# The low half of split weights made by GpSimd instead of an accumulating DMA, and the indexer's dots taken one head at a time

## What is computed

```python
for l in range(DEPTH):                      # 2 layers, x: (1, 512, 1024)
    x = x + 0.5 * swiglu(rms_norm(x, ffn1_norm[l]), ffn1_gate[l], ffn1_up[l], ffn1_down[l])   # 1024 -> 2816 -> 1024
    h = rms_norm(x, mix_norm[l])
    aq, ak, av, iq, ik, iw, pu, mq = jnp.split(h @ w_in[l], IN_OFFSETS, axis=-1)
    # A: sparse attention, 8 heads x 64. The indexer (4 heads x 64) scores every key:
    #    score[t,s] = sum_h iw[t,h]/2 * relu(iq[t,h] . ik[s] / 8), s <= t
    #    each query keeps the 128 keys of the largest score and attends to them
    # B: causal pooling over trailing windows 2, 4, 8, 16, a small map per group
    # C: attention of 4 heads to 256 memory tokens
    x = x + jnp.concatenate([y_attn, y_pool, y_mem], axis=-1) @ w_out[l]
    x = x + 0.5 * swiglu(rms_norm(x, ffn2_norm[l]), ffn2_gate[l], ffn2_up[l], ffn2_down[l])
```

## Time and profile before

| | us |
|---|---|
| median of 3 runs | 1982.85 (1980.84 to 1983.37) |
| the profiled execution's own time | 1983.37 |
| its span in the profile | 1981.4 |
| TensorE busy | 1948.7 (98%) |
| ScalarE busy | 1086.5 (55%) |
| VectorE busy | 617.1 (31%) |
| GpSimd busy | 350.7 (18%) |
| w_lo<-raw: DMAs issued, us to landing | 328, 5.7 |

### The profile page before, as it was taken

One profiled execution on the slowest core, in us unless ns is written; L12 is line 12 of the kernel. 1 busy time (PEld: TensorE's weight loads), 2 busy tenths in 40 slices (PEclk: granted clock), 3 DMA queues, 4 the chain that ended last, 5 costly groups with the idle time before them and its releaser, 6 DMA issues.

```text
span 1981.4 us, 27709 instructions
## 1 busy us (share of the span) xinstructions
PE 1948.7 (98%) x9256; PEld 1571.9 (79%) x9256; DVE 617.1 (31%) x1180; ACT 1086.5 (55%) x1393; POOL 350.7 (18%) x404
## 2 busy tenths in 40 slices
PE   6999999999999999999999999999999999999999
PEld 4888888886768888888878888888767688888887
DVE  3222200367662322220052222004676532222101
ACT  6655543563584655553375565336546666565432
POOL 1111111111431111111111111111116111111111
PEclk9999999999999999999999999999999999999999
DMA  7988888887336888888878888888762379888886
GB/s 217 218 188 192 195 190 194 190 192 176 83 87 144 195 188 190 193 194 194 195 170 200 189 186 199 196 195 200 185 155 54 87 170 206 194 197 189 195 195 180
DMA packets 97799, 354.54 MB, mean 179 GB/s; under 512 B 11000, under 2 KB 11256, under 8 KB 97472
## 3 DMA queue, kind: packets, MB, share of 16 engines
q0 software_dynamic: 47232, 171.99, 48.7%
q1 hardware_dynamic: 49824, 178.84, 27.5%
q10 hardware_dynamic: 672, 2.80, 0.4%
HBM read 179.52 MB, written 2.10 MB: 92 GB/s over the span
## 4 chain that ended last, share of the span: by engine, by line
PE 97%; DMA 1%; ACT 1%; issue 1%; DVE 0%; SPq 0%; DVEq 0%; ACTq 0%; POOLq 0%
PE bank L453 95%; PE bank L806 2%; DMA w_lo<-raw 1%; DMA x<-x_t 0%; ACT w_lo L920 0%; ACT prob L1066 0%; DVE pt L336 0%; ACT a_hi L1082 0%; ACT t L1066 0%; DVE t L1323 0%; DVE x L1150 0%; DVE z L1277 0%; ACT pt L1059 0%; ACT mv L1046 0%; DVE yt L1341 0%
## 5 line engine op out<-in xcount | busy, mean ns | idle before, releaser
L919 ACT ACTIVATE w_hi<-raw 128x1024 fp32r<-128x1024 f32 x329 | 349.0, 1061 | 645.5 <-PE bank L453 630.8
L453 PE MATMUL bank<-h_hi,w_hi 128*128 128x512 f32 x1664 | 654.6, 393 | 15.9 <-ACT h_hi L891 13.9
L453 PE MATMUL bank<-h_hi,w_lo 128*128 128x512 f32 x1664 | 649.5, 390 | 5.6 <-DMA w_lo<-raw 5.6
L453 PE MATMUL bank<-h_lo,w_hi 128*128 128x512 f32 x1664 | 632.9, 389 | 0.0
L385 POOL DMA_DIRECT2D w_lo<-raw x328 | 283.5, 866 | 1589.6 <-ACT w_lo L920 1549.7
L453 PEld LDWEIGHTS bank<-h_hi,w_hi 128*128 128x128 f32 x1664 | 313.3, 188 | 97.5 <-ACT h_hi L891 15.3
L453 PEld LDWEIGHTS bank<-h_hi,w_lo 128*128 128x128 f32 x1664 | 313.3, 188 | 71.3 <-DMA w_lo<-raw 6.1
L453 PEld LDWEIGHTS bank<-h_lo,w_hi 128*128 128x128 f32 x1664 | 312.4, 188 | 65.5 <-issue 1.2
L920 ACT ACTIVATE w_lo<-raw 128x1024 fp32r<-128x1024 f32 x329 | 343.5, 1044 | 0.0
L453 PE MATMUL bank<-a_hi,w_hi 128*128 (+2 forms) x864 | 334.1, 387 | 0.0
L453 PE MATMUL bank<-a_lo,w_hi 128*128 (+2 forms) x864 | 332.8, 385 | 0.0
(11 more groups left out here) (138 smaller groups left out, 1273.9 us busy)
## 6 DMA issues: line engine op xcount, KB each, us to landing
raw<-weights SPq DMA_DIRECT2D x332, 512.0 KB, 4.6
w_lo<-raw POOLq DMA_DIRECT2D x328, 512.0 KB, 5.7
x<-x_t SPq DMA_DIRECT2D x4, 512.0 KB, 7.3
mem<-mem_t ACTq DMA_DIRECT2D x2, 1024.0 KB, 7.1
out_t<-x SPq DMA_DIRECT2D x8, 256.0 KB, 2.1
const<-consts SPq DMA_DIRECT2D x1, 505.5 KB, 10.1
spread_in<-spreads ACTq DMA_DIRECT2D x2, 216.0 KB
wpool<-pool_w ACTq DMA_DIRECT2D x2, 128.0 KB, 7.0
```

What stands on the lines that cost most here:

```text
L453: return nc.tensor.matmul(out_, lhsT, rhs, start=start, stop=stop, skip_group_check=True)
L919: nc.scalar.activation(w_hi[:, s], raw[:, s], ACT.Copy).then_inc(w_hi_done, 1)
```

## The change

w_lo is no longer made by a negating ScalarE pass and an accumulating DMA, but by one GpSimd `tensor_tensor` that subtracts w_hi from raw. One semaphore `w_ready` counts the slots in order, in place of four. The dots of the indexer are no longer paired nor put between the v blocks: they run head by head, before project_v(2), in two banks, and from the third on each waits for a relu. ROUNDS_AT is gone: each of the ten evacuations is followed by one round, and FIRST_ROUNDS is 6 instead of 2.

```diff
-ROUNDS_AT = (1, 1, 1, 1, 1, 1, 2, 2, 2, 2)
-FIRST_ROUNDS = ROUNDS - sum(ROUNDS_AT)
+FIRST_ROUNDS = ROUNDS - ZT
...
                 if not first:
-                    sp.wait_ge(w_ready[pos], 16 * rounds)
+                    sp.wait_ge(w_ready, n + (1 - RING))
...
-                wait_apart(pool, w_neg_done, l * SLOTS + n[0] + (n[1] + 1))
-                G.dma_start(w_lo[:, s], raw[:, s], accum_op=ALU.add).then_inc(w_ready[pos], 16)
+                pool.wait_ge(w_hi_done, l * SLOTS + n[0] + (n[1] + 1))
+                G.tensor_tensor(out=w_lo[:, s], in0=raw[:, s], in1=w_hi[:, s].bitcast(f32),
+                                op=ALU.subtract).then_inc(w_ready, 1)
...
-                def project_v(s, before=None):
-
+                def project_v(s):
                     n = at("av", s)
-                    lo_ready_of(l, n)
+                    pe.wait_ge(w_ready, l * SLOTS + (n + 1))
...
-                def dots(i):
-
-                    if i >= 2:
-                        pe.wait_ge(relu_ready, l * 12 + (i - 1) * IDX_HEADS)
-                    for hp in range(0, IDX_HEADS, 2):
-                        at_q = (hp // 2) * T + i * P
-                        for part, (tq, tk) in enumerate(((idx_hi, idx_hi), (idx_hi, idx_lo),
-                                                         (idx_lo, idx_hi))):
-                            for half in range(2):
-                                p = slice(half * HD, (half + 1) * HD)
-                                last = mm(bank[hp + half][:, 0:(i + 1) * P], tq[p, at_q:at_q + P],
-                                          tk[p, 2 * T:2 * T + (i + 1) * P], part == 0, part == 2)
-                                if part == 2:
-                                    last.then_inc(dots_done[half], 1)
...
+                n = 0
                 pe.wait_ge(idx_lo_ready, (l + 1) * 3)
-                pe.wait_ge(cols_ready, l + 1)
-                project_v(2, {(0, 0): 1, (1, 1): 2})
-                project_v(3, {(0, 2): 3})
+                for i in range(1, TT):
+                    for h in range(IDX_HEADS):
+                        if n >= 2:
+                            pe.wait_ge(relu_ready, l * 12 + (n - 1))
+                        p0 = HD * (h % 2)
+                        at_q = (h // 2) * T + i * P
+                        q = [t[p0:p0 + HD, at_q:at_q + P] for t in (idx_hi, idx_lo)]
+                        k = [t[p0:p0 + HD, 2 * T:2 * T + (i + 1) * P] for t in (idx_hi, idx_lo)]
+                        passes(bank[n % 2][:, 0:(i + 1) * P], q, k, True, True)\
+                            .then_inc(dots_done, 1)
+                        n += 1
+                project_v(2)
+                project_v(3)
...
                 nc.scalar.activation(w_hi[:, s], raw[:, s], ACT.Copy).then_inc(w_hi_done, 1)
-                nc.scalar.activation(w_lo[:, s], raw[:, s], ACT.Copy, scale=-1.0)\
-                    .then_inc(w_neg_done, 1)
...
-                        act.wait_ge(dots_done[h % 2], l * 6 + (n // 2 + 1))
+                        act.wait_ge(dots_done, l * 12 + (n + 1))
...
-                        nc.scalar.activation(chunk(t2, n % 2, T, (i + 1) * P), bank[h][:, 0:(i + 1) * P],
+                        nc.scalar.activation(chunk(t2, n % 2, T, (i + 1) * P), bank[n % 2][:, 0:(i + 1) * P],
...
-                    for _ in range(ROUNDS_AT[j]):
-                        take_largest(l * DVE_CHAIN + links[0])
-                        links[0] += ROUND_CHAIN
+                    take_largest(l * DVE_CHAIN + links[0])
+                    links[0] += ROUND_CHAIN
```

More of the change, by code:

```diff
@@ L208, in build @@
     w_hi_done = sem("w_hi_done")
-    w_neg_done = sem("w_neg_done")
-    w_ready = [sem(f"w_ready{i}") for i in range(RING)]
+    w_ready = sem("w_ready")
     slot_done = sem("slot_done")
@@ L249, in build @@
     idx_lo_ready = sem("idx_lo_ready")
[L250 removed]
+    dots_done = sem("dots_done")
     relu_ready = sem("relu_ready")
@@ L346, in _, with load @@
         def _(sp):
-            def load(n, pos, rounds=0, first=False):
+            def load(n, pos, first=False):
                 if not first:
-                    sp.wait_ge(w_ready[pos], 16 * rounds)
+                    sp.wait_ge(w_ready, n + (1 - RING))
                 src = weights[ds(n, 1), :, :].rearrange("a p n -> (a p) n")
@@ L446, in _ @@
         def _(pe):
-            def lo_ready_of(l, n, off=0):
-                pe.wait_ge(w_ready[n % RING], 16 * (SLOTS // RING) * l + off * (16 // RING)
-                           + 16 * (n // RING + 1))
             def mm(out_, lhsT, rhs, start=True, stop=True):
@@ L538, in gate_up @@
                     pe.wait_ge(gu_free, (l * 2 + e) * FC + (f + (half + 1)))
+                    at = l * SLOTS + ffn_at + f * 2 + 2 * half
                     for up in range(2):
                         pos = (n + up) % RING
-                        lo_ready_of(l, n + up, f * 2)
+                        pe.wait_ge(w_ready, at + (up + 1))
                         for k in range(DC):
@@ L558, in down @@
                 def down(f, off, start=False, stop=False, **part):
[L559 to L562 removed]
+                    at = l * SLOTS + down_at + f + off
+                    pe.wait_ge(w_ready, at + 1)
                     pe.wait_ge(a_lo_ready, (l * 2 + e) * FC + (f + (off + 1)))
@@ L604, in mix @@
                 pe.wait_ge(rms_ready, l * 3 + 2)
-                def v_block(n, s, half, i):
-                    k = 2 * s + half
-                    hhi, hlo = pair(h_hi, h_lo, k * T + i * P, P)
-                    return passes(bank[4 + i][:, :], (hhi, hlo), weight(n % RING, half * T, T),
-                                  k == 0, k == DC - 1)
-                def project_v(s, before=None):
+                def project_v(s):
                     n = at("av", s)
-                    lo_ready_of(l, n)
+                    pe.wait_ge(w_ready, l * SLOTS + (n + 1))
                     for half in range(2):
+                        k = 2 * s + half
+                        whi, wlo = weight(n % RING, half * T, T)
                         for i in range(TT):
-                            if before is not None and (half, i) in before:
-                                dots(before[half, i])
-                            last = v_block(n, s, half, i)
+                            hhi, hlo = pair(h_hi, h_lo, k * T + i * P, P)
+                            last = passes(bank[4 + i][:, :], (hhi, hlo), (whi, wlo),
+                                          k == 0, k == DC - 1)
                     last.then_inc(slot_done, 1)
-                def dots(i):
-                    if i >= 2:
-                        pe.wait_ge(relu_ready, l * 12 + (i - 1) * IDX_HEADS)
-                    for hp in range(0, IDX_HEADS, 2):
-                        at_q = (hp // 2) * T + i * P
-                        for part, (tq, tk) in enumerate(((idx_hi, idx_hi), (idx_hi, idx_lo),
-                                                         (idx_lo, idx_hi))):
-                            for half in range(2):
-                                p = slice(half * HD, (half + 1) * HD)
-                                last = mm(bank[hp + half][:, 0:(i + 1) * P], tq[p, at_q:at_q + P],
-                                          tk[p, 2 * T:2 * T + (i + 1) * P], part == 0, part == 2)
-                                if part == 2:
-                                    last.then_inc(dots_done[half], 1)
                 project_v(0)
```

28 lines of the change are left out of this document (12 added, 16 removed).

## The result

| | before | after |
|---|---|---|
| median us | 1983.11 (1980.84 to 1986.96, 4 runs) | 2014.22 (2013.38 to 2014.52, 4 runs) |
| span of the profiled execution | 1981.4 | 2012.2 |
| mean granted clock | 0.996 | 0.985 |
| ScalarE, GpSimd, VectorE busy | 1086.5, 350.7, 617.1 | 788.7, 891.2, 755.7 |

The ratio is 1.0154, 95% interval 1.0141 to 1.0167: 31 us slower. The forecast was 2013.

The account below looks back on a forecast made before the run. The prediction took TensorE's nearly gapless matmuls as the bound, with time decided at six seams, the dots and attention. Its terms summed to +30.3 on 1983.4, 2013.7, as a median 2013 us; range 1988 to 2024.

Parts of the forecast that it names:

- The port: At the seams, GpSimd's SBUF-reading subtraction of about 2.4 us excludes VectorE's two-input adds of squares, and TensorE waits.
- the mix seams: Mix seam in each layer: two subtractions inside VectorE's adds stall TensorE 4.3 us each, +8.6 in all.
- the second feed-forward's: Second feed-forward's seam in each layer: one subtraction falls among the adds, 1.9 us each, +3.8 in all.
- between the layers: Seam between the layers: the low-half wait of 1.99 us goes, but two subtractions delay the adds, +3.3 us.
- The start: Kernel start: the low half comes earlier, but subtractions hold VectorE's adds, so -2.8 us and not -6.5.
- the fourth rival: Waits worse: clock falls at every seam and the start, a subtraction hits the accumulations; another +3.4 to +12 us; 17%.
- The clock behind idle stretches: After mix-seam and between-layer idle stretches TensorE's clock falls; two of three falls counted, +6.8 us.
- The dots: Indexer dots head by head before v: held by relu and accumulation, 20.0 us against 15.2, +9.6 in all.
- The prediction's lower bound for it: Order of the dots: at least 3.3 us a layer, from 36 matmuls of unpaired halves with no wait.
- The clock is the term: Clock fall in the half-row dots, partly covered by waits: 2.0 us a layer (0 to 3.4), +4.0 in all.
- The rounds: Six top-k rounds before the first evacuation: hidden with 4 us of cover, cost 0.
- The attention: Attention units: ScalarE loses four negation passes a layer, gaining 1.5 us of at most 3.8 a layer, -3.0 in all.

Follow-up runs that it names:

- write_only: The changed kernel with GpSimd's subtraction replaced by zero fills of the same place, which read nothing: 1985.11 us.
- after_fix: The changed kernel with GpSimd waiting at the seams for VectorE's last add, and four banks for the dots instead of two: 1982.89 us, ratio 1.0008.
- tt_only: The kernel before with only the GpSimd subtraction in place of negation and DMA, dots and rounds untouched: 1998.05 us, ratio 1.0079.
- rounds_only: The kernel before with only the top-k rounds changed, six ahead of the first evacuation and one behind each: 1994.17 us, ratio 1.0055.

## Why the prediction was right

- **The port, first of all.** "The first waits for the add under way and then goes ahead of the next add": so it was, at all six seams, and write_only leaves the reading as what counts. The Trainium skill (SBUF — State Buffer, "Who interferes with whom") has the rule that a VectorE instruction with two SBUF inputs contends with a GpSimd one that reads SBUF, and not with one that only writes it. The trace agrees with both halves: 3.30 us for an add of 1.23 beside subtractions, 3.54 and 0.69 for the adds beside fills. The adds were held by 2.05 each (5.63 - 3.55 = 2.08, 2.72 - 0.69 = 2.03) and not by 2.40, the whole subtraction. At the mix seam the subtraction ended 2.26 us after the first add did, and the add that it held ended 1.07 after that instead of 1.23, which is most of the other 0.35. With the 0.5 us of slack that makes 3.65 at the mix seams instead of 4.3 and 1.6 at the second feed-forward's instead of 1.9; between the layers it was 2.4 instead of 3.3.
- **The start.** -3.6 up to the matmul of sums against -2.8, but with a fall of the clock, which began 1.6 us before that matmul and cost 2.55 behind it. It stood only in the fourth rival. Together -1.0.
- **The clock behind idle stretches.** 6.9 against 6.8, but by luck, for the members are others. The prediction had "I take two of the three" at 3.4 each; the clock fell at all three (1.2, 1.2, 1.9) and at the start (2.55). The 1.5 us of waiting at the second feed-forward brought no fall.
- **The dots.** The order alone cost at most 4.25 a layer at full clock (19.46 - 15.21) against 4.8. The prediction's lower bound for it, 3.3 for "unpaired halves with no wait", is too high: heads still overlap, and with four banks layer 0 lost 2.7 (17.89 - 15.21). The accumulations were hit once, by the subtraction that began at 421.23: the first took 0.93 instead of 0.48, with the next ones free. The clock is the term that was mis-sized: 4.65 and 4.25 against "2.0 a layer, partly covered by waits", over the upper end of its 0 to 3.4. What failed is the length of the fall. The prediction took the 6.8 us of the earlier trace rows, worth 3.4, and left 2.0 of it uncovered; it lasted 13.7 us in each layer, worth 6.8. The cover was about as good as reckoned, 2.2 to 2.6 us of it. In layer 0 about half of the cost came in the dots (10.95 us instead of 8.56) and half in v (+2.3): the low stretch reached 4.6 us into the v matmuls (437.4 against 432.8), where nothing covers it.
- **The rounds.** 0, as predicted, and the cover was needed: with the same rounds and the old dots it is 3.9 us and a fall of the clock in each layer. The cover was larger than the 4 us reckoned. The scores came 13.2 us after the first dot instead of 11.2, but v ended 24.1 after it instead of 20.0. after_fix, with 18.4, has no such wait either. That the subtraction might hold a round is not borne out either. VectorE's and GpSimd's rows after the change, both engines at once:

```profile
442.40 0.07 DVE L1221 MATCH_VALUE_LOAD score<-top,score 128x8 f32 x1
442.46 0.68 DVE L1221 MATCH_REPLACE8 score<-top,score 128x512 f32<-128x512 f32 x1
```

```profile
441.94 2.41 POOL L383 TENSOR_TENSOR w_lo<-raw,w_hi 128x1024 fp32r<-128x1024 f32 x1 [18.36 <-ACT w_hi L903]
```

  The replacement takes its 0.68 in the middle of the subtraction.
- **The attention.** -3.1 against -3.0, but the agreement is partly luck: in layer 0 (-2.2) the clock was low for 3.4 us instead of 6.8, which makes 1.7 of it. In layer 1, with equal falls, the relief of ScalarE was worth 0.9, not 1.5. Whether the shorter fall comes from the relief isn't settled: it was 3.4 in some layers and 6.8 in others in kernels with and without the negation.

The sum, +30.3 against +30.8, is closer than its terms: the adds at the seams (15.7 against 13.0) and the order of the dots (9.6 against 8.5) were put 3.8 too high, the clock (10.8 against 15.8) 5.0 too low. The mechanisms were right, but that the total is off by only half a microsecond is luck.

## What to carry to other kernels

Before work that reads SBUF is moved to GpSimd, look for the places where VectorE runs a chain of operations with two SBUF inputs, each waiting for the one before, that TensorE waits for: each such link let one GpSimd operation in ahead here, and cost nearly its whole length (2.05 us of 2.40). Everywhere else the operation was free here, so hold back only those slots with one more wait; that turned +15 us into -6. Be careful with long runs of matmuls on half of the rows. Paired and spread among full ones, as in the kernel before, they kept 2.4 GHz, though not in every kernel (tt_only: 3.4 us at 1.2 GHz in each layer). Read the granted clock over such a stretch before its waits: here the clock cost about as much as the order. And read it over several executions, for one profile can show a fall that most don't have, or miss one that most have.

## What was not expected of the hardware

- The port goes back and forth between operations: three subtractions of 2.40 took 10.32 us (3.1 more) beside three adds that lost 4.1. A fill of the same place cost the adds nothing. At these seams GpSimd got in only where VectorE waited for itself. A subtraction that waited from 1018.53, while VectorE was making h_lo, let the first add through, which follows without a wait and took its 2.29 us, and ended 2.21 us behind it.
- TensorE was granted 1.2 GHz for 13.7 us a layer in the dots and behind them while its longest wait was 0.6 us, and for 27.3 us in one execution in which 15 of 51 matmuls were of full rows; two other executions of that kernel kept the clock up.
- The waits of 3.5 to 5.5 us at the seams, and those of 3.9 in rounds_only, each went with 3.4 or 6.8 us at 1.2 GHz, which began between 3 us before the end of the wait and 1 us after it. The 5.57 us at the start of the kernel before had none with it.
